# Down projection of the second block's first feed-forward as seven half products per 2x2 group

## The reference, cut to what matters

```python
def conv_ffn(h, w_up, w_conv, b_conv, w_down):
    u = dwconv_centred(h @ w_up, w_conv, b_conv)
    g, v = jnp.split(u, 2, axis=-1)
    return (jax.nn.silu(g) * v) @ w_down
...
        h_lat = h_lat + ga2 * conv_ffn(f_lat, w_ffn_up[i], w_ffn_conv[i], b_ffn_conv[i], w_ffn_down[i])
        if not last:
            h_ctx = h_ctx + cga2 * conv_ffn(f_ctx, w_ffn_up[i], w_ffn_conv[i], b_ffn_conv[i], w_ffn_down[i])
```

## Time and profile before

| | |
|---|---|
| median of 3 runs | 2651.49 us (2650.31 to 2652.76) |
| span of the profiled execution | 2649.1 us |
| TensorE busy with matmuls | 2552.1 us, 96% |
| VectorE busy | 1718.7 us, 65% |
| ScalarE busy | 1056.5 us, 40% |
| first down projection of the stage | 1646.2 to 1737.8 us |
| second one | 1920.7 to 2012.3 us |

### The profile page before, as it was taken

One profiled execution on the slowest core, in us unless ns is written; L12 is line 12 of the kernel. 1 busy time (PEld: TensorE's weight loads), 2 busy tenths in 40 slices (PEclk: granted clock), 3 DMA queues, 4 the chain that ended last, 5 costly groups with the idle time before them and its releaser, 6 DMA issues.

```text
span 2649.1 us, 32136 instructions
## 1 busy us (share of the span) xinstructions
PE 2552.1 (96%) x13096; PEld 2130.9 (80%) x13096; DVE 1718.7 (65%) x2364; ACT 1056.5 (40%) x1455; POOL 24.3 (1%) x31
## 2 busy tenths in 40 slices
PE   7998999999999999999989999999999999999998
PEld 6887788888778888777768888888888787788887
DVE  6886798887688877768534655235534686663563
ACT  4546442233454245443442433123324564442342
POOL 0000000000100000000000000000000000000000
PEclk9999999999899999999999999999999999999999
DMA  8432388654145666211102122211211111233232
GB/s 287 168 120 75 99 291 299 214 187 143 53 135 192 207 197 222 84 61 47 62 9 64 49 64 65 71 56 64 73 63 56 56 45 44 80 97 103 96 97 87
DMA packets 90658, 296.69 MB, mean 112 GB/s; under 512 B 9216, under 2 KB 23168, under 8 KB 90256
## 3 DMA queue, kind: packets, MB, share of 16 engines
q1 hardware_dynamic: 90512, 294.64, 34.1%
HBM read 289.88 MB, written 2.10 MB: 110 GB/s over the span
## 4 chain that ended last, share of the span: by engine, by line
PE 85%; DVE 9%; ACT 3%; issue 2%; DMA 1%; SPq 0%; DVEq 0%; ACTq 0%
PE ps L372 69%; PE ps L400 3%; PE ps L3534 1%; PE ps L3209 1%; PE ps L974 1%; PE ps L3177 1%; DVE gatt L1003 1%; DMA spare<-in_ada_w 1%; PE ps L3190 1%; PE ps L2556 1%; DVE w_lo L353 1%; PE ps L590 1%; PE ps L1981 1%; ACT w_hi L345 0%; DVE spare L504 0%
## 5 line engine op out<-in xcount | busy, mean ns | idle before, releaser
L372 PE MATMUL ps<-h_hi,w_hi 128*128 128x512 f32 (+1 forms) x2344 | 784.4, 371 | 9.4 <-DVE w_lo L353 6.4
L372 PE MATMUL ps<-h_lo,w_hi 128*128 128x512 f32 (+1 forms) x2344 | 775.2, 367 | 0.0
L372 PE MATMUL ps<-h_hi,w_lo 128*128 128x512 f32 (+1 forms) x2344 | 774.9, 367 | 0.0
L353 DVE TENSOR_TENSOR w_lo<-w_raw,w_hi 128x1024 fp32r<-128x1024 f32 (+2 forms) x318 | 412.3, 1297 | 429.4 <-ACT w_hi L345 428.4
L345 ACT ACTIVATE w_hi<-w_raw 128x1024 fp32r<-128x1024 f32 (+2 forms) x318 | 355.2, 1117 | 737.2 <-PE ps L372 686.1
L372 PEld LDWEIGHTS ps<-h_hi,w_hi 128*128 128x128 f32 x2344 | 440.6, 189 | 90.6 <-DVE w_lo L353 11.0
L372 PEld LDWEIGHTS ps<-h_hi,w_lo 128*128 128x128 f32 x2344 | 442.4, 189 | 73.9
L372 PEld LDWEIGHTS ps<-h_lo,w_hi 128*128 128x128 f32 x2344 | 442.6, 189 | 72.9 <-issue 1.4
L372 PE MATMUL ps<-g_hi,w_hi 128*128 128x512 f32 (+1 forms) x880 | 295.7, 369 | 0.8 <-DVE w_lo L353 0.8
L372 PE MATMUL ps<-g_hi,w_lo 128*128 128x512 f32 (+1 forms) x880 | 294.8, 368 | 0.0
L372 PE MATMUL ps<-g_lo,w_hi 128*128 128x512 f32 (+1 forms) x880 | 294.8, 368 | 0.0
(11 more groups left out here) (460 smaller groups left out, 2705.9 us busy)
## 6 DMA issues: line engine op xcount, KB each, us to landing
w_raw<-in_up SPq DMA_DIRECT2D x176, 512.0 KB, 3.5
m_raw<-in_w_mod SPq DMA_DIRECT2D x96, 512.0 KB, 3.5
w_raw<-in_down SPq DMA_DIRECT2D x64, 704.0 KB, 4.1
m_raw<-in_ada_w SPq DMA_DIRECT2D x57, 512.0 KB, 4.7
w_raw<-in_in SPq DMA_DIRECT2D x39, 512.0 KB, 3.5
spare<-in_ada_w SPq DMA_DIRECT2D x24, 512.0 KB, 4.5
w_raw<-in_out SPq DMA_DIRECT2D x16, 512.0 KB, 3.4
w_raw<-in_qkv SPq DMA_DIRECT2D x12, 512.0 KB, 3.5
```

The costliest lines, as they stand in the source:

```text
L353: dve.tensor_tensor(low, raw_weights(k, g), high.bitcast(F32), ALU.subtract).then_inc(*k.tick("w_lo", g))
L372: last = pe.matmul(k.ps[:, product_bank(g, bank) if place is None else place, 0:tn], a[:, c, :], b[:, c, t0:t0 + tn], start=c == 0 and n = ...
```

## The change

**The scheme.** For this one down projection the 2816 inner features are taken in portions of 8, 8 and 6 tiles instead of 11 and 11. Within a portion, output tiles are taken in pairs (`p` = 0 to 3), inner tiles in pairs of an even and an odd one, tokens in two halves of 384 (`EARLY`, `LATE`): a 2x2 by 2x2 block product. It is made with seven products instead of eight. On the weights' side the operands are A11, A12, A21, A22 (row = output tile of the pair, column = the even or the odd inner tiles) and four sums of them, S1 to S4; on the side of the gated values B11, B21, B22 and four sums, T1 to T4. Each half product `q` (28 in a portion, `STEPS`) is `pairs` x 3 matmuls of 384 columns, where `pairs` is 4, 4 and 3.

**TensorE.** The seven products of a pair of output tiles go to three banks: four of them (A11, S2, S3, A22) into one bank, one on top of the other, S1 and S4 into a second, A12 alone in a third; two sets of banks alternate. The running content of a bank is added into `x` after each product (`dve_partial`), and the next product into the same bank waits for that read-out (`a1`, `a2`, `a3`, `e1`). For `p` = 0 the products of S2 and A12 change places. At the head of a portion, the products 2 and 3 are split so that the last pair of inner tiles comes later (`early`, `late`).

**ScalarE and VectorE.** Each product's weights get a high and a low part, in five slots (`SLOT_OF`) that lie over the weight buffers; slots 0 to 2 are free after the last but one up tile, 3 and 4 after the last one. VectorE makes S1 to S4, and for each pair of inner tiles T1 to T4 and their low parts. In iteration `q` it reads out product `q - 4` (`LEAD`), makes the weight sum of product `q + 1` if that has one, and the low part of product `q`. In iteration 28 it also makes the low part of the next up tile's weights.

**Loads.** A row of down weights (one output tile, 512 KB or 384 KB) goes to `w_raw` or, for the second row of odd pairs, to `w_other`, which lies over the convolution's buffers. The first row of a pair is fetched after S4 of the pair before.

**Places.** `g_hi` and `g_lo` of this stage become `comb_hi` and `comb_lo`, 7 operands of 384 columns for each pair of inner tiles. The host cuts the down weights to fit (`down10_0` to `down10_2`). The load semaphores of `x` are renamed to `loaded`. The rest of the program is unchanged.

The diff, cut to its core; left out are the copies of the up stage's helpers (same operations and shapes as before, other tiles), the high and low parts (`act_weights_high`, `dve_weights_low`, `act_g_high`, `dve_g_low`: one operation each behind its waits) and the places.

```diff
--- before.py
+++ after.py
...
+PORTIONS = ((0, 8), (8, 16), (16, 22))
...
-    ffn(1, 0)
+    for n, (first, end) in enumerate(PORTIONS):
+        run(("up", 1, 0, n), "up10", 2 * first, 2 * (end - first))
+        run(("down", 1, 0, n), f"down10_{n}", 0, KD, end - first)
...
+        self.w_other = Place(nc, scratch_at, "_10")("w_other", [P, KD * P])
...
+        self.slot_hi = [piece(f"slot_hi{i}", high + o, dt=F32R) for i, o in enumerate((4096, 8192, 18432, 0, 10240))]
+        self.slot_lo = [piece(f"slot_lo{i}", high + o, dt=F32R) for i, o in enumerate((6144, 16384, 20480, 2048, 12288))]
+        self.slot_sum = [piece(f"slot_sum{i}", high + o) for i, o in enumerate((6144, 16384, 20480, 2048, 12288))]
+        self.second_sum = piece("second_sum", high + 14336)
...
+PRODUCTS = (("A11", "B11", "A"), ("S1", "T1", "E"), ("S2", "T2", "A"), ("A12", "B21", "B"), ("S3", "T3", "A"), ("S4", "B22", "E"), ("A22", "T4", "A"))
+OPERANDS = ("B11", "T1", "B21", "B22", "T2", "T3", "T4")
+STEPS = len(PRODUCTS) * KD // 2
+SLOT_OF = [0, 1, 2, 3, 4] * 5 + [0, 3, 4]
+LEAD = 4
...
+def product_of(q):
+    p, m = divmod(q, len(PRODUCTS))
+    return p, {2: 3, 3: 2}.get(m, m) if p == 0 else m
+def fold_product(n, q):
+    down = BASE["down", 1, 0, n]
+    return ("product", {STEPS - 3: down + KD - 2, STEPS - 1: down + KD - 1}.get(q, ("fold", n, q)))
+def slot_free(n, q):
+    down = BASE["down", 1, 0, n]
+    before = [i for i in range(q) if SLOT_OF[i] == SLOT_OF[q]]
+    if before:
+        return fold_product(n, before[-1])
+    return "product", down - 2 if SLOT_OF[q] < 3 else down - 1
+def fold_bank(p, role):
+    return {"A": (4, 0), "E": (5, 1), "B": (6, 7)}[role][p % 2]
+def row_tile(k, n, p, row):
+    g = BASE["down", 1, 0, n] + 2 * p + row
+    if row and p % 2:
+        return k.w_other, "loaded1", g
+    return k.w_raw[g % 2], f"w_load{g % 2}", g
...
+def added(n, p, what):
+    down = BASE["down", 1, 0, n]
+    return ("taken", {"e2": down + 2 * p, "a4": down + 2 * p + 1}.get(what, ("fold", n, p, what)))
+ADDED = ("a1", "e1", "a2", "b", "a3", "e2", "a4")
+def sp_row(k, n, p, row):
+    sp, down = k.nc.sync, BASE["down", 1, 0, n]
+    tile, name, g = row_tile(k, n, p, row)
+    if row == 0 and p == 0:
+        sp.wait_ge(*k.seen("w_lo", down - 2))
+    elif row == 0:
+        sp.wait_ge(*k.seen("folded", ("S4", n, p - 1)))
+        sp.wait_ge(*k.seen("w_lo", ("fold", n, 7 * (p - 1) + (3 if p > 1 else 2))))
+    elif p == 0:
+        sp.wait_ge(*k.seen("w_lo", down - 1))
+    elif p == 1:
+        sp.wait_ge(*k.seen("gated", down - 1))
+    else:
+        sp.wait_ge(*k.seen("w_lo", ("fold", n, 7 * (p - 2) + 6)))
+    kt = count_of(n)
+    sp.dma_start(tile[:, 0:kt * P], k.ins[f"down10_{n}"][2 * p + row, :, :]).then_inc(*k.tick(name, g, 16))
...
+def sp_fold(k):
+    for n in range(len(PORTIONS)):
+        up = BASE["up", 1, 0, n]
+        for t in range(2 if n else 3, 2 * count_of(n)):
+            sp_fetch(k, up + t)
+        for p, row in ((0, 0), (0, 1), (1, 1), (1, 0), (2, 1), (2, 0), (3, 1), (3, 0)):
+            sp_row(k, n, p, row)
+        for i in range(2):
+            sp_after_fold(k, n, i)
+    sp_fetch(k, QKV + 2)
+def pe_fold_product(k, n, q, part=None, first=True, last=True):
+    pe, pairs, (p, m) = k.nc.tensor, count_of(n) // 2, product_of(q)
+    _, operand, role = PRODUCTS[m]
+    down = BASE["down", 1, 0, n]
+    if first:
+        pe.wait_ge(*k.seen("w_lo", ("fold", n, q)))
+        if m == 0 and p >= 2:
+            pe.wait_ge(*k.seen(*added(n, p - 2, "a4")))
+        if m == 0 and p == 1:
+            pe.wait_ge(*k.seen("taken", down - 1))
+        if m in (2, 4, 5, 6):
+            pe.wait_ge(*k.seen(*added(n, p, {2: "a1", 4: "a2", 5: "e1", 6: "a3"}[m])))
+    o = OPERANDS.index(operand)
+    wh, wl = k.slot_hi[SLOT_OF[q]], k.slot_lo[SLOT_OF[q]]
+    for i in range(pairs) if part is None else part:
+        if p == 0 and i == pairs - 1:
+            pe.wait_ge(*k.seen("g_lo", (1, 0, PORTIONS[n][1] - 1 - (operand in ("B11", "T1")), operand if operand[0] == "T" else "B")))
+        th, tl = k.comb_hi[i][:, o, :], k.comb_lo[i][:, o, :]
+        ah, al = wh[:, i * P:(i + 1) * P], wl[:, i * P:(i + 1) * P]
+        for turn, (a, b) in enumerate(((ah, th), (ah, tl), (al, th))):
+            op = pe.matmul(k.ps[:, fold_bank(p, role), 0:HALF_T], a, b, start=m in (0, 1, 3) and i == 0 and turn == 0,
+                           stop=i == pairs - 1 and turn == 2, skip_group_check=True)
+    if last:
+        op.then_inc(*k.tick(*fold_product(n, q)))
+def pe_fold(k):
+    for n in range(len(PORTIONS)):
+        up, pairs = BASE["up", 1, 0, n], count_of(n) // 2
+        if n == 0:
+            pe_pair(k, up, TALL, k.h_hi, k.h_lo, rms_parts(1), apart=True)
+        for t in range(0 if n else 2, 2 * count_of(n)):
+            pe_product(k, up + t, TALL, k.h_hi, k.h_lo)
+        early, late = range(pairs - 1), range(pairs - 1, pairs)
+        pe_fold_product(k, n, 0)
+        pe_fold_product(k, n, 1)
+        pe_fold_product(k, n, 2, early, last=False)
+        pe_fold_product(k, n, 3, early, last=False)
+        pe_fold_product(k, n, 3, late, first=False)
+        pe_fold_product(k, n, 2, late, first=False)
+        for q in range(4, STEPS):
+            pe_fold_product(k, n, q)
+    pe_sums(k, ("rms", 2))
...
+def dve_weights_sum(k, n, p, name):
+    dve, width, down = k.nc.vector, count_of(n) // 2 * P, BASE["down", 1, 0, n]
+    m = {"S1": 1, "S2": 2, "S3": 4, "S4": 5}[name]
+    q = 7 * p + ({2: 3}.get(m, m) if p == 0 else m)
+    lo = k.slot_sum[SLOT_OF[q]][:, 0:width]
+    a11, a12, a21, a22 = (quad(k, n, p, a) for a in ("A11", "A12", "A21", "A22"))
+    second = k.second_sum[:, 0:width]
+    if name != "S2":
+        dve.wait_ge(*k.seen(*slot_free(n, q)))
+    if name == "S1":
+        for row in range(2):
+            dve.wait_ge(*row_loaded(k, n, p, row))
+        op = dve.tensor_tensor(lo, a21, a22, ALU.add)
+    elif name == "S2":
+        dve.wait_ge(*k.seen("folded", ("S1" if p else "S3", n, p)))
+        if p:
+            op = dve.tensor_tensor(second, k.slot_sum[SLOT_OF[7 * p + 1]][:, 0:width], a11, ALU.subtract)
+        else:
+            op = dve.tensor_tensor(second, a22, k.slot_sum[SLOT_OF[4]][:, 0:width], ALU.subtract)
+    elif name == "S3":
+        op = dve.tensor_tensor(lo, a11, a21, ALU.subtract)
+    else:
+        dve.wait_ge(*k.seen("folded", ("S2", n, p)))
+        op = dve.tensor_tensor(lo, a12, second, ALU.subtract)
+    op.then_inc(*k.tick("folded", (name, n, p)))
...
+def dve_partial(k, n, q, gates):
+    dve, (p, m) = k.nc.vector, product_of(q)
+    tile = 2 * p + (m in (1, 4, 6))
+    tokens = ((0, CTX, 0), (CTX, HALF_T, 1)) if m in (0, 3, 6) else ((HALF_T, TALL, 1),)
+    base = 0 if m in (0, 3, 6) else HALF_T
+    dve.wait_ge(*k.seen(*fold_product(n, q)))
+    for t0, t1, seg in tokens:
+        x = k.x[:, tile, t0:t1]
+        op = dve.scalar_tensor_tensor(x, k.ps[:, fold_bank(p, PRODUCTS[m][2]), t0 - base:t1 - base], gates(tile)[seg], x, ALU.mult, ALU.add)
+    op.then_inc(*k.tick(*added(n, p, ADDED[m])))
...
+def dve_turned(k, n, j, what):
+    dve, even, odd, turn1, turn4 = k.nc.vector, k.g10[0], k.g10[1], k.turn1[:, :], k.turn4[:, :]
+    dve.wait_ge(*(k.seen("folded", ("T2", n, j)) if what == "T4" else k.seen(*gated_key(n, j))))
+    if what == "T1":
+        op = dve.tensor_tensor(turn1, even[:, LATE], even[:, EARLY], ALU.subtract)
+    elif what == "T2":
+        op = dve.tensor_tensor(turn1, odd[:, LATE], turn1, ALU.subtract)
+    elif what == "T3":
+        op = dve.tensor_tensor(even[:, LATE], odd[:, LATE], even[:, LATE], ALU.subtract)
+    else:
+        op = dve.tensor_tensor(turn4, odd[:, EARLY], turn1, ALU.subtract)
+    op.then_inc(*k.tick("folded", (what, n, j)))
...
+def g_parts(j):
+    return ("B", "T2", "T3", "T4") if j % 2 else ("B", "T1")
+def act_fold(k):
+    for n in range(len(PORTIONS)):
+        up, tiles10, end, rms = BASE["up", 1, 0, n], 2 * count_of(n), PORTIONS[n][1], n == len(PORTIONS) - 1
+        for t in range(tiles10):
+            if t == tiles10 - 1:
+                for q in range(3):
+                    act_weights_high(k, n, q)
+            elif n or t:
+                act_split(k, up + t + 1)
+            if t:
+                act_up10(k, n, t - 1)
+            if t and t % 2 == 0:
+                for what in g_parts(PORTIONS[n][0] + t // 2 - 1):
+                    act_g_high(k, n, PORTIONS[n][0] + t // 2 - 1, what)
+        act_up10(k, n, tiles10 - 1)
+        act_weights_high(k, n, 3)
+        for what in g_parts(end - 1):
+            act_g_high(k, n, end - 1, what)
+        if rms:
+            act_tables(k)
+        for q in range(4, STEPS):
+            act_weights_high(k, n, q)
+            if rms and q >= 10 and q % 7 in (3, 4):
+                act_square(k, ("rms", 2), 2 * (q // 7) - 2 + (q % 7 == 4), BASE["down", 1, 0, n])
+        act_split(k, BASE["down", 1, 0, n] + KD)
+    down = BASE["down", 1, 0, len(PORTIONS) - 1]
```

(70 more changed lines are left out.)

127 lines of the change are left out of this document (121 added, 6 removed).

## The result

The changed kernel takes **2666.4 us** (median of 9 runs, 2663.36 to 2668.1) against 2652.56 us for the kernel before on the same chip (9 runs, 2648.99 to 2660.9). The ratio is **1.0048, interval 1.0035 to 1.0061**: slower by 0.48%. The profiled execution has a span of 2665.9 us, before 2649.1: +16.8. The forecast was +19.3 on that span, and 2671 us.

A forecast was written before the change was run, and what follows sets the result against it. TensorE, busy 96% of the span, was taken as the bound. -22.9 + 2 x (7.2 + 2.4) + 16.0 + 1.9 = +14.2 us, with the clock's +5.1 together +19.3: 2671 us, range 2653 to 2685 (leaving out 2 in 10).

The forecast's parts named there:

- rival 1: Whole kernel: the clock stays at 2.4 GHz despite the waits, +14.2 us, 2666 us; chance 0.14.
- The gain: TensorE in the down projection: 924 matmuls of 384 columns replace 528 pairs, -22.9 us (-16.7 at 0.18 us each).
- The head of a portion of 8: First products of each portion of 8: TensorE waits 2.7, 0.9 and 2.65 us at products 4, 5, 6; 7.2 with small waits.
- The tail: End of each portion of 8: product 25 waits 1.25 us and product 27 waits 1.1, together 2.4 us.
- The portion of 6: Last portion: VectorE is the bound, stalls of 16.0 us (head 10.6); the normalisation behind it comes 1.9 us later.
- (d): Sign in the last portion: it has nearly half of the loss, and VectorE runs there without a pause.
- The clock: Clock falls to 0.50 behind long waits, in three heads and at product 25: three of four charged, +5.1 us (0 to 10).
- The up projections: Added sums and low parts in the up projections, 33 us of work, are hidden and cost nothing.
- Sign (b): TensorE idle some 35 us in the three portions; each head has three waits for VectorE, of 2.7, 0.9 and 2.7 us.
- Rival 2: Only the three heads cost; tails and the VectorE-bound stretch hide: +2 us, 2654 us; chance 0.11.
- Rival 3: VectorE's small pieces in SBUF cost half, so stalls shrink: -8 us, 2643 us; chance 0.07.
- Rival 4: Stalls feed on each other through queued row loads, all clock falls come, 384 columns take 0.18 us: past 2685 us; chance 0.10.

The follow-up runs named there:

- e4: Changed kernel with the read-out of product 4 moved ahead of S1, low 7 and S2 in VectorE's queue: 2664.42 us.
- e6: Changed kernel with filler matmuls of ones, which nobody reads, ahead of products 4 and 6: 2666.82 us.
- e2: Changed kernel with other weight slots for the last products, product 26 taking slot 3 from product 21 instead of product 23: 2663.0 us.
- e1: Changed kernel with the read-out of product 25 ahead of the split of the next up tile's weights on VectorE: 2663.37 us.
- e3: Changed kernel with work left out: sums of squares of tiles 2 to 6 made for 8 columns only: 2663.46 us.
- e10: e8 with a cyclic slot order, low of T3 behind read-out 3, and tile 6's square ahead of the last read-out: 2640.76 us, ratio 0.9936 to the kernel before.
- e5: Changed kernel with the high part of product 4's weights ahead of the last g tile's four high parts on ScalarE: 2665.91 us.
- e0: The changed kernel again, unaltered, measured beside e10 and the kernel before on one chip: 2668.43 us, ratio 1.0044 to the kernel before.
- e8: Changed kernel with the reorderings of e1, e2, e4 and e5, T4 and its low part later, and the table load earlier: 2651.15 us.
- e9: e8 with the sums of squares of the RMS norm behind the stage made by GpSimd instead of VectorE: 2646.93 us.

## Why the prediction was right, and where it was not

The forecast, slower by over 0.2%, came true, at 2666 instead of 2671 us. That is also the time of rival 1, but not its mechanism: the clock did fall. That the sum came so near is in part luck, since two errors have opposite signs: the clock was charged at 5.1 us and cost 1.7, and the attention gave 1.3 us that stood in no term. Point by point:

- **The gain, -22.9 us.** Right. Starts are 0.173 us apart in unbroken runs, and 924 of them are 160.15 us. The upper bound of 0.18 has no row.
- **The head of a portion of 8, 7.2 us.** Right in size and in its links: the read-out of product 3 was done 11.7 us behind the last up product (11.8 predicted), product 4 waited 2.67 (2.7), the row was there at 16.7 (17.0), product 6 started at 19.3 (19.7). e4 showed the second link by taking S1 from in front of the read-out. The wait at product 5 wasn't seen in after, since product 4 ran at half clock; e6 brought it out, at 0.73 (0.9).
- **The tail, 2.4 us.** Right: 1.21 + 1.17. e2 showed the slot as the cause of the first, e1 the split as that of the second.
- **The portion of 6, 16.0 us, and 1.9 ahead of the sums.** Waits of 1.84 + 0.65 (2.8 predicted), 3.86 (3.85), 2.26, 0.63 (0.7), 3.07 (3.1) and 1.69 (1.65), 14.0 in all, and 1.87 ahead of the sums (1.9). Two clock falls fill the stretch up to 17.8: the first, 1.65 us, stood in place of product 5's wait and of a part of product 6's (1.4 + 2.55 predicted, 1.65 + 2.26 measured), the second came on top. e3 confirmed the part that is VectorE's load. But "VectorE is the bound" said too much: it is busy for 49.8 of 63.3 us, and e10 does the portion in 53.2 with 48.9 us of nearly the same work. Half of the loss (10.1 of 19.6 us, one fall of the clock less among them) was order there too, and (d), VectorE without a pause, was wrong: in front of its part of the split it was idle for 2.04 us.
- **The clock, +5.1 us.** This is the term that was mis-sized. The stage had four falls in the profiled execution. The sums by stretch show the two of the last portion; the first pair of lines is product 4's wait and what follows, the second product 6's.

```profile
1973.90:1977.50 3.60, 0.00 (x0) 0.02 (x1) 1.69 (x4) 1.85 (x3) 0.00 (x0) 1.00 0.00 0
1977.60:1980.90 3.30, 3.30 (x11) 3.19 (x12) 2.71 (x11) 0.94 (x2) 0.00 (x0) 0.50 0.13 34
1981.00:1984.30 3.30, 1.45 (x9) 1.12 (x7) 2.35 (x5) 1.44 (x3) 0.00 (x0) 1.00 0.60 194
1984.40:1987.70 3.30, 3.16 (x10) 3.19 (x11) 1.46 (x3) 1.28 (x3) 0.00 (x0) 0.50 0.01 2
```

Only the last of the four falls lengthened anything, by about 1.7 us. The prediction had the rule (a fall behind the first long wait is absorbed, behind the second it is lost) and then charged three as if each came where it is lost. Where a fall comes is not fixed by the program: e3, e5 and e0 had falls behind product 6 in a portion of 8, and the fourth place that the prediction named, product 25 of the portion of 6, had one in e6 and e0 (1.3 and 1.4 us) and none in after. The same program paid 1.7 us in after's profiled execution and 3.0 in e0's. Charged by the rule, the profiled execution comes to +16 of the predicted +19.3.
The Trainium skill's rule cited with the prediction ("TensorE: Matmul & The Clock Gate", section "Loop structure matters more than you think") says that a copy out of PSUM on VectorE leaves the matmuls warm where the next matmuls follow immediately. It can't be carried over to this kernel, where TensorE waits 2.5 us for the read-out: the clock fell around product 4 of both portions of 8 in after, e1, e2 and e4.
- **The up projections, nothing.** Right: 133.1 and 99.9 us without a gap, in every run.
- **Sign (b), TensorE idle for some 35 us.** The stretches of after show 27.1 us (6.3 + 6.3 + 14.5), over the 23 that would have refuted the prediction. The rest of the 35 is there in other forms: by an estimate from the rows above, some 18 restarts of 0.17 us count as busy, and three falls at 1.65 us each filled waits.

Summed again with what was measured: -22.9 + 2 x (7.1 + 2.35) + 17.8 + 1.9 = +15.7 us, where the stage shows +15.5. The whole span has 1.3 us more than the stage. It arises in the attention, where a clock fall came at another wait than in the earlier trace rows; this was read from the trace only and not tested.

Rival 2 (only the heads cost) falls with the tails' measured 2.4 us and the portion of 6. Rival 3 (pieces in SBUF cost half) falls with 0.55 us for 384 columns, on the line of the earlier trace rows. Rival 4 needed every fall to be lost and matmuls at 0.18 us. What the prediction did not ask was whether its stalls were of load or of order. By its own walk VectorE was late in the head because of the sequence in which it did things, and e10 gets 24.4 us of the stage back by sequence and choice of slots alone. What is left over the full rate is 2.3 us in each portion of 8 and 9.5 in that of 6; how much of that VectorE's load keeps, no run shows.

## What to carry to other kernels

A scheme that trades matmuls for sums on another engine pays at its seams: count the waits of the first and last few steps of each portion before the steady rate, and order each engine's queue by the time at which TensorE asks for each piece. When a read-out frees a bank or a slot, nothing that waits for a load or for another engine may stand in front of it. Remove such waits together. Alone, e1 and e4 kept what they won (1.2 and 1.7 us in a portion of 8), e2 gave 0.8 of 1.2 us back at another wait, and e5's 1.2 us was lost to a fall of the clock; together they gave 24.4 us (e10).

## What the hardware showed that was not expected

- The granted clock fell from 1.00 to 0.50 (from 2.4 to 1.2 GHz) during or behind TensorE's waits for VectorE, and stayed there for 3.4 us, or for 6.8 (portion of 6 in e1, e3 and e0). The waits were mostly of 2.1 to 3.7 us, but in e8, e9 and e10 the fall came 8 us into the portion of 6, where TensorE had been idle for 1.67 and 0.49 us only (the two lines of e10 below). The same waits don't always bring one: after those two there was none in e5 and e6, and at the 2.9 us ahead of product 25 in the portion of 6 there was a fall in e6 and e0 and none in after, e1, e4 and e5. Its price is 0 or some 1.3 to 1.7 us, by whether a wait follows.

```profile
1948.53:1956.50 7.97, 5.82 (x32) 5.17 (x31) 7.47 (x14) 4.77 (x7) 0.00 (x0) 1.00 0.16 49
1956.60:1959.90 3.30, 3.30 (x11) 2.98 (x11) 2.98 (x7) 1.04 (x2) 0.00 (x0) 0.50 0.00 0
```

- VectorE's two-source pieces in SBUF are held until a two-source sum of GpSimd ends (0.55 us becomes 1.54 to 2.20), while its read-outs of PSUM are not.
- A sum of 768 columns takes GpSimd 1.84 us and VectorE 0.95.
